# The keys' squares of each head in two rounded parts, summed by two fp32r matmuls instead of one plain fp32 matmul

## What is computed

```
def rmsnorm_2(x, gain):
    xf = x.astype(jnp.float32)
    inv = lax.rsqrt(jnp.mean(xf * xf, axis=-1, keepdims=True) + NORM_EPS)
    return (xf * inv * gain.astype(jnp.float32)).astype(x.dtype)
...
    k_nope, v = kv[..., :QK_NOPE_DIM], kv[..., QK_NOPE_DIM:]
    k_pe = jnp.broadcast_to(k_rope_raw[:, :, None, :], (B, L, N_HEADS, QK_ROPE_DIM))
    k = jnp.concatenate([k_nope, k_pe], axis=-1)
    q = rmsnorm_2(q, g_qn)
    k = rmsnorm_2(k, g_kn)
```

## Time and profile before

| | |
|---|---|
| median of three runs | 3097.29 us (3096.9 to 3099.05) |
| the profiled execution | 3097.21 us, its span 3095.4 us |
| PE busy | 2998.0 us, 97% of the span |
| DVE, ACT, POOL busy | 1431.8, 741.8, 1113.2 us (46%, 24%, 36%) |
| head stages of the two layers start at | about 1668.5 and 2626 us |
| granted TensorE clock, mean | 0.992 of full speed |

### The profile page before, as it was taken

The page is one execution under the profiler, slowest core; times in us unless marked ns, Lnnn a source line. Parts: engine busy times, 40 slices in busy tenths (PEclk is TensorE's granted clock), DMA queues, the critical chain, the costliest instruction groups (busy, mean ns, idle before and its releaser), DMA issues.

```text
span 3095.4 us, 41490 instructions
## 1 busy us (share of the span) xinstructions
PE 2998.0 (97%) x16430; PEld 2679.9 (87%) x16430; DVE 1431.8 (46%) x1801; ACT 741.8 (24%) x1299; POOL 1113.2 (36%) x1335
## 2 busy tenths in 40 slices
PE   7999899999999999999999999999999999999999
PEld 5777787888888888999998888899999999788899
DVE  3796864332222249300115666657510022666761
ACT  3144430000000023001112555402000111555500
POOL 3652144444444454433333111144533434111132
PEclk9999999999999999999999999999999999999999
DMA  2111111111111112112111000331212112000142
GB/s 113 48 34 38 68 55 49 48 47 47 44 45 46 53 42 105 54 47 98 48 69 63 15 15 14 119 116 69 83 48 104 42 54 90 21 15 15 42 166 82
DMA packets 46727, 183.68 MB, mean 59 GB/s; under 512 B 6000, under 2 KB 6128, under 8 KB 46064
## 3 DMA queue, kind: packets, MB, share of 16 engines
q1 hardware_dynamic: 31248, 113.19, 10.8%
q10 hardware_dynamic: 15328, 68.33, 5.8%
HBM read 150.58 MB, written 30.91 MB: 59 GB/s over the span
## 4 chain that ended last, share of the span: by engine, by line
PE 91%; DVE 5%; ACT 1%; issue 1%; POOL 1%; DMA 0%; ACTq 0%; DVEq 0%; POOLq 0%
PE acc L483 67%; PE aux L1097 4%; PE acc L981 4%; PE acc L1076 4%; PE acc L589 3%; PE acc L1030 2%; PE acc L965 1%; PE acc L1003 1%; PE acc L993 1%; DVE act_lo L1838 1%; POOL w_lo L411 0%; PE acc L1014 0%; DMA residual<-in_xT 0%; DVE work L1877 0%; PE acc L1034 0%
## 5 line engine op out<-in xcount | busy, mean ns | idle before, releaser
L411 POOL TENSOR_TENSOR w_lo<-w_raw,w_hi 128x256 fp32r<-128x256 f32 (+1 forms) x924 | 851.9, 954 | 17.2
L483 PE MATMUL acc<-act_hi,w_hi 128*128 128x348 f32 (+1 forms) x2896 | 708.4, 345 | 23.4 <-issue 8.3
L483 PE MATMUL acc<-act_lo,w_hi 128*128 128x348 f32 (+1 forms) x2896 | 706.4, 344 | 0.0
L483 PEld LDWEIGHTS acc<-act_hi,w_hi 128*128 128x128 f32 x2896 | 504.9, 188 | 68.0 <-issue 21.8
L483 PE MATMUL acc<-act_hi,w_lo 128*128 128x348 f32 (+1 forms) x2896 | 561.9, 344 | 0.0
L483 PEld LDWEIGHTS acc<-act_lo,w_hi 128*128 128x128 f32 x2896 | 506.6, 188 | 39.1
L431 POOL TENSOR_TENSOR small<-shape_consts 128x1 f32<-128x1 f32 x192 | 46.0, 239 | 1344.1 <-PE acc L483 1242.8
L483 PEld LDWEIGHTS acc<-act_hi,w_lo 128*128 128x128 f32 x2896 | 490.2, 188 | 39.5
L483 PE MATMUL acc<-ff_split,w_hi 128*128 128x512 f32 (+1 forms) x1376 | 314.0, 375 | 3.3 <-DVE ff_split L1838 3.2
L483 PEld LDWEIGHTS acc<-ff_split,w_hi 128*128 128x128 f32 x1376 | 246.8, 188 | 50.2 <-DVE ff_split L1838 4.3
L2129 DVE TENSOR_TENSOR residual<-acc,residual 128x1024 f32<-128x1024 f32 (+1 forms) x82 | 100.7, 1228 | 370.2 <-PE acc L483 370.1
(11 more groups left out here) (298 smaller groups left out, 3809.9 us busy)
## 6 DMA issues: line engine op xcount, KB each, us to landing
w_raw<-in_wstream SPq DMA_DIRECT2D x215, 512.0 KB, 3.2
spill_x<-residual ACTq DMA_DIRECT2D x2, 4176.0 KB, 12.3
spill_m<-residual ACTq DMA_DIRECT2D x2, 4176.0 KB, 13.5
spill_g<-work ACTq DMA_DIRECT2D x16, 522.0 KB, 2.7
residual<-spill_m ACTq DMA_DIRECT2D x16, 522.0 KB, 5.8
work<-spill_g ACTq DMA_DIRECT2D x16, 522.0 KB, 8.8
residual<-spill_x ACTq DMA_DIRECT2D x16, 522.0 KB, 4.2
residual<-in_xT ACTq DMA_DIRECT2D x8, 512.0 KB, 9.9
```

What stands on the lines that cost most here:

```text
L411: ins = nc.gpsimd.tensor_tensor(Wl[:, s, c0:c0 + w], Wraw[:, s, c0:c0 + w], Wh[:, s, c0:c0 + w].bitcast(F32), ALU.subtract)
L483: ins = nc.tensor.matmul(acc[0:m, s, p, 0:w], wt[:, ws, w0 + j * m:w0 + j * m + m], x[:, k, p * w:p * w + w], start=(first and t == 0), st ...
```

## The change

The keys' squares are now held as two fp32r tiles `k_sq`: a rounded part and its remainder. `ones96` gets an fp32r copy, `ones96_r`. `key_sum` is two fp32r matmuls, ones by rounded part and ones by remainder, that add up in `acc_n`. `query_sum` stays as it was.

- ACT squares the key rows twice: once in fp32 into a scratch place of X, once rounded into `k_sq[0]`.
- DVE gets a step for each piece, `key_square_low`, at n = 1, 6 and 11 of the round: scratch less rounded part, into `k_sq[1]`. `key_sum` waits for it, and so does the next piece's first square.
- In the round h = -1, `key_sum` stands at n = 3, 8, 13 instead of 2, 7, 12.
- Once per layer, DVE splits the rotary squares (64 x 1044) after chunk 7, and makes `ones96_r`.
- `rope_tmp` moves to another place in SBUF.

```diff
+        ones96_r = G_[:, extra0:extra0 + P]
+        k_sq = tuple(G_[:, 6 * RW + TP * i:6 * RW + TP * i + TP] for i in range(2))
+        rope_tmp = X_[:, 6 * TP + QP:6 * TP + 2 * QP]
...
                 def key_sum(g, pc):
                     pe.wait_ge(*n_free[0])
-                    pe.wait_ge(sems["k_squared"], k)
-                    nc.tensor.matmul(acc_n[:, 0:w], ones96, X[:, 6, c0:c0 + w], start=True,
-                                     stop=True).then_inc(sems["k_sum"], 1)
+                    pe.wait_ge(sems["k_square_low"], k)
+                    for i in range(2):
+                        ins = nc.tensor.matmul(acc_n[:, 0:w], ones96_r, k_sq[i][:, c0:c0 + w], start=(i == 0), stop=(i == 1))
+                    ins.then_inc(sems["k_sum"], 1)
...
-                            if n in (2, 7, 12):
+                            if n in ((3, 8, 13) if h < 0 else (2, 7, 12)):
                                 key_sum(g, n // 5)
...
-                    do(nc.scalar.activation(X[top, 6, c0:c0 + w], acc_n[top, 0:w], ACT.Square), "k_squared")
+                    if k > 1:
+                        act.wait_ge(sems["k_square_low"], k - 1)
+                    nc.scalar.activation(X[top, 6, 0:w], acc_n[top, 0:w], ACT.Square)
+                    do(nc.scalar.activation(k_sq[0][top, c0:c0 + w], acc_n[top, 0:w], ACT.Square), "k_squared")
...
                     split(R[:, 8 + j, wide], Ah[:, j, :], Al[:, j, :], "a_ready")
+                    if j == 7:
+                        split(X[rr, 6, :], k_sq[0][rr, :], k_sq[1][rr, :], "dve_step")
...
+                do(vec.tensor_copy(ones96_r, ones96))
...
+                def key_square_low(g, pc):
+                    dve.wait_ge(sems["k_squared"], k)
+                    do(vec.tensor_tensor(k_sq[1][top, own], X[top, 6, 0:w], k_sq[0][top, own].bitcast(F32),
+                                         ALU.subtract), "k_square_low")
...
+                        if more and n in (1, 6, 11):
+                            key_square_low(g, n // 5)
```

More of the change, by code:

```diff
@@ L221, in build @@
         extra0 = idr0 + 3 * P + 34 * TB
-        assert extra0 + QP <= 8 * RW
-        rope_tmp = R_[:, 8 * RW + extra0:8 * RW + extra0 + QP]
+        ones96_r = G_[:, extra0:extra0 + P]
+        k_sq = tuple(G_[:, 6 * RW + TP * i:6 * RW + TP * i + TP] for i in range(2))
+        assert extra0 + P <= 6 * RW and 2 * TP <= 2 * RW
+        rope_tmp = X_[:, 6 * TP + QP:6 * TP + 2 * QP]
         head_inv = tuple(R[:, 18, QP * i:QP * i + QP] for i in range(2))
@@ L317, in build @@
             "spilled", "m_spilled", "g_spilled", "g_spilled_late", "stored", "pos_in", "t_spilled", "t_in",
-            "kv_raw", "q_raw", "k_free", "q_free", "k_squared", "q_squared", "k_sum", "q_sum", "kn_free", "qn_free",
+            "kv_raw", "q_raw", "k_free", "q_free", "k_squared", "q_squared", "k_square_low", "k_sum", "q_sum", "kn_free", "qn_free",
             "rs_k", "rs_q", "k_normed", "q_normed", "k_hi", "q_hi", "k_lo", "q_lo",
@@ L2360, in query_table @@
                     do(vec.tensor_tensor(q[rope, 0:w], q[rope, 0:w], rope_tmp[rope, 0:w], ALU.add))
+                def key_square_low(g, pc):
+                    k = wave(l, g, pc)
+                    c0, w = QP * pc, piece_width(pc)
+                    own = slice(c0, c0 + w)
+                    dve.wait_ge(sems["k_squared"], k)
+                    do(vec.tensor_tensor(k_sq[1][top, own], X[top, 6, 0:w], k_sq[0][top, own].bitcast(F32),
+                                         ALU.subtract), "k_square_low")
                 def query_norm(g, pc):
```

## The result

The changed kernel takes 3113.56 us (median of six runs, 3108.52 to 3116.76), the kernel before 3097.1 us in the same comparison. The ratio is 1.0059, with an interval of 1.0048 to 1.0069: slower by 0.6%, 15 to 21 us, where the forecast was 11. The direction and the mechanism of the steady rounds were right; the sum for the round h = -1 was too small, and 1.0059 times the old median is just above the end of the stated range.

What follows compares the result with a forecast made beforehand. PE bounds the kernel, except where it waits for DVE's chains ahead of blocks 7 and 12 and in round h = -1. Steady rounds +3.4 us and h = -1 +7.5 us make +10.9 on 3097.2: 3108 us, range 3100 to 3115.

Steps and rivals of the forecast that it cites:

- the two rounds h = -1: Round before each layer's steady rounds: nothing hides a delay; 4.0 us in layer 1, 3.5 in layer 0, +7.5 us.
- step 1: Round h = -1, piece 0: keys' sum waits for DVE's subtraction; values_in, queries' sum, next L965 and query_table 1.9 us later.
- the clock: Rival: longer waits in h = -1 may bring more stretches at 1.2 GHz; two more per layer give 3112 us; chance 0.06.
- PE's part: Keys' sums on PE: fp32r pairs save 0.30, 0.30 and 0.22 us, 0.82 us per head, 11.5 us over 14 steady rounds.
- DVE's part: Steady round: subtraction at block 1 costs nothing, at blocks 6 and 11 lengthens the round by 0.59 and 0.47 us.
- ACT's part: Steady round: one more square per piece, 0.51 us at 384 columns, fits with 0.2 us left at block 1.
- Ahead of the heads: DVE's split of rotary squares, up to 2.4 us, fits into 2.6 us of waits at chunks 0 to 2; costs nothing.
- Steps 2 to 4: Round h = -1, layer 1, after piece 0's keys' sum: rough scores 2.9, then 3.3 us later; 4.0 us at the end.
- the DVE chains are covered, wholly or in part: Rivals: PE's saving alone, 3084 us, 0.07; one subtraction exposed, 3101 us, 0.13; both covered, h = -1 slower, 3093 us, 0.07.
- the pair is no cheaper: Rival: two fp32r matmuls cost as much as the plain keys' sum; +13.1 us, 3121 us; chance 0.02.

Runs made afterwards that it cites:

- e1: The changed kernel, but in the steady rounds DVE subtracts for pieces 1 and 2 directly behind query_norm instead of ahead: 3100.74 us, ratio 1.0017.
- e8: The kernel before plus only DVE subtractions at blocks 1, 6 and 11 of steady rounds, on constants, result unread: 3110.58 us, ratio 1.0039.
- e4: The changed kernel with the plain sum for head 0 and, in steady rounds, subtractions of pieces 1 and 2 behind query_norm: 3088.35 us, ratio 0.9974.
- e9: The changed kernel, but GpSimd splits head 1's weights only after the first query_norm of the round h = -1: 3109.27 us, ratio 1.0048.

## Why the prediction was right or wrong

What failed is the term for the two rounds h = -1: 7.5 us forecast, 11.6 measured, because its step 1 was mis-sized and the clock was left out of it.

- **PE's part: right.** 0.82 us per steady round were forecast, and e1 against the kernel before measures 0.81. The trace of e1 has the pair at 0.52 us with its tail.
- **DVE's part: right in place and size.** 0.59 + 0.47 = 1.06 us forecast; 1.05 and 1.09 us measured. The subtraction of block 1 cost nothing. A steady round was to grow by 0.24 us and grew by 0.24.
- **ACT's part: right.** The additional square cost nothing that can be seen; with it in place, e1 keeps PE's whole saving.
- **Ahead of the heads: nearly right.** The split of the rotary squares went into DVE's waits of chunks 0, 1 and 2, as forecast, but DVE's last split then ended 0.26 us later against PE's first product. I had put that at nothing.
- **The round h = -1, step 1: too small by 1.0 us in each layer.** I took the lengths of a cast and a subtraction from rows of the steady rounds with no weight split of POOL beside them. At this place it splits weights, and DVE's instructions are longer: cast and copy 0.79 us for 0.4, the subtraction 0.80 for 0.56, and the 0.26 us of the last split come on top, 0.9 of the 1.0 us. The evidence stood in my own rows: L1838 with 1.67 us in the earlier trace rows, which I used as an upper bound for another edit and did not question here. Steps 2 to 4 were right given step 1, to some 0.3 us. Makes 2.0 us.
- **The round h = -1, the clock: wrong place in the sum.** I put longer stretches at the low clock among the rivals, with 0.06, and took layer 1 at the clock it had before. It fell from 0.94 to 0.77, 1.9 us in this pair of traces, of which 1.0 is also the difference between two executions of the unchanged round (e8's layer 1). For layer 0 I took 0.5 us off, and 0.3 it was. The rival was not another outcome beside the forecast but a part of it: the change made PE wait longer in a round that already ran partly at the low clock, and paid for that too. The earlier trace rows did not show that the stretch with longer waits had the lower clock: PE is idle there for 26.50 - 21.13 = 5.4 us at 0.84 in layer 0, and for 7.0 us at 0.94 in layer 1. Nor are the 0.9 us between the layers in these rows, whose stretches I had cut myself; 30.93 against 29.97 us bears them out. Makes 2.1 us with layer 0.
- **The sum.** 7.5 + 2.0 + 2.1 = 11.6 us for the two rounds, and 14 x 0.24 = 3.4 us: 15.0 us by the traces, against 10.9 forecast and 15 to 21 us measured. The range ended at 3115 us, too near, because its upper bound had the clock but not the longer DVE steps, and not both together. A slip without effect: by the prediction's own 0.35 and 0.25 us for two products, pricing one at 0.163 us would save 0.9 us more over the 14 rounds and not 0.3; e1's 0.81 us per round agrees with the rows.
- **The rivals.** That the DVE chains are covered, wholly or in part, is refuted by e1 and e8. That the pair is no cheaper is refuted by e1.

## What to carry to other kernels

A cheaper instruction on the busiest engine pays only in the stretches where that engine is last. The helper step that it needs was paid in full here where it stood ahead of what that engine waits for, and cost nothing that can be seen where it stood behind it: the same two subtractions, moved behind `query_norm` in the same queue, turned +0.24 us per round into -0.81 us. The round that fills the pipeline had no cover, and it was best left as it was (e4). Read the lengths for its sum from rows with the same neighbours at work, POOL's among them, and reckon with its clock.

## What the runs showed of the hardware

- PE ran nine additional plain matmuls per layer and the kernel before became faster by 0.15% (0.9985, 0.9976 to 0.9994): the granted clock in the round h = -1 went from 0.83 and 0.94 to 1.00, and the round from 30.9 and 30.0 to 28.4 us.
- Beside POOL's subtractions (5.13 us for four of 128 x 256) DVE's SBUF to SBUF instructions take longer, subtractions with two sources as well as casts: 128 x 1044 1.67 for 1.25 and 1.12 for 0.70 us, 128 x 128 0.64 for 0.23 us, 64 x 384 0.80 for 0.56 us. Each is longer by 0.24 to 0.42 us. POOL's four take 2.97 us in e9, where less of DVE's work lies beside them.
